# Row-cut transposes in the mixture-of-experts loop: seven of eight transposes of a 64-slot block work on 64 rows

## The reference, cut to what matters

```
for each expert e, over its tokens (rows of h, gathered):
    gu   = xb @ w_e1[e] + b_e1[e]            # 1024 -> 2048
    gate = min(gu[:, :1024], 7);  up = clip(gu[:, 1024:], -7, 7)
    act  = (up + 1) * (gate * sigmoid(1.702 * gate))
    y    = act @ w_e2[e] + b_e2[e]           # 1024 -> 1024
```

## Time and profile before

| | |
|---|---|
| median of 3 runs | 1825.05 us (1824.0 to 1827.08) |
| the profiled execution, its own time | 1826.37 us |
| its span in the trace | 1824.1 us |
| TensorE busy | 1649.4 us (90%), 6773 matmuls and transposes |
| TensorE weight loads busy | 1213.6 us (67%) |
| VectorE / ScalarE busy | 1387.1 us (76%) / 1049.0 us (58%) |
| the chain that ended last | TensorE 62%, VectorE 18%, issue 10%, ScalarE 7% |
| mean granted clock of TensorE | 0.954 |

### The profile page before, as it was taken

How to read it: one execution, slowest core, us unless ns; L and a number is a source line. 1 busy time by engine, 2 the same in 40 slices (tenths; PEclk the granted TensorE clock), 3 DMA queues, 4 the chain that set the end, 5 groups by cost and what they waited for, 6 DMA issues and landing times.

```text
span 1824.1 us, 20657 instructions
## 1 busy us (share of the span) xinstructions
PE 1649.4 (90%) x6773; PEld 1213.6 (67%) x6773; DVE 1387.1 (76%) x1198; ACT 1049.0 (58%) x1038; POOL 313.2 (17%) x301
## 2 busy tenths in 40 slices
PE   2999989988898389999999999999999999999872
PEld 2776667766677367667777776777777766777640
DVE  7878756656547757898889889889889889888626
ACT  2456822556423245677668667767767767766511
POOL 1600000100000102223123132132222312312000
PEclk8999989999998599999999999999999999999985
DMA  8333255312155269999999999999999999999435
GB/s 324 111 139 139 81 179 191 97 47 70 47 215 220 79 245 366 400 408 400 388 402 413 382 391 415 385 384 416 382 373 416 388 375 405 391 378 397 181 146 233
DMA packets 112255, 519.82 MB, mean 285 GB/s; under 512 B 15666, under 2 KB 48978, under 8 KB 57906
## 3 DMA queue, kind: packets, MB, share of 16 engines
q1 hardware_dynamic: 97168, 492.99, 68.8%
q0 software_dynamic: 10208, 17.64, 2.8%
q10 hardware_dynamic: 4834, 8.60, 1.3%
HBM read 514.46 MB, written 19.66 MB: 293 GB/s over the span
## 4 chain that ended last, share of the span: by engine, by line
PE 62%; DVE 18%; issue 10%; ACT 7%; DMA 2%; POOL 2%; ACTq 0%; DVEq 0%; POOLq 0%
PE ps L2125 28%; PE ps L2141 13%; PE ps L1832 9%; DVE lo L1686 7%; PE ps L2042 2%; PE ps L2057 2%; PE ps L2097 2%; ACT hi L1092 2%; POOL gw L622 1%; DVE acc L1235 1%; PE ps L2112 1%; PE ps L1921 1%; ACT hi L860 1%; PE ps L2105 1%; ACT prob L981 1%
## 5 line engine op out<-in xcount | busy, mean ns | idle before, releaser
L1686 DVE TENSOR_TENSOR lo<-raw,hi 128x2048 fp32r<-128x2048 f32 x318 | 716.8, 2285 | 156.5 <-ACT hi L1092 156.5
L1092 ACT ACTIVATE hi<-raw 128x2048 fp32r<-128x2048 f32 x318 | 596.9, 1911 | 231.5 <-PE ps L2125 217.3
L2125 PE MATMUL ps<-hi,x_a 128*128 128x512 f32 x864 | 242.9, 411 | 0.0
L1832 PE MATMUL ps<-hT,hi 128*128 128x512 f32 x704 | 231.4, 404 | 10.4 <-DVE qbd L1445 8.5
L753 POOL TENSOR_TENSOR ticks<-eps 128x1 f32<-128x1 f32 x100 | 75.6, 756 | 738.2 <-ACT ysb L1129 709.2
L2125 PEld LDWEIGHTS ps<-hi,x_a 128*128 128x128 f32 x864 | 162.7, 191 | 42.0 <-issue 9.4
L1832 PEld LDWEIGHTS ps<-hT,hi 128*128 128x128 f32 x704 | 133.5, 190 | 46.5 <-issue 16.2
L2125 PE MATMUL ps<-hi,x_b 128*128 128x512 f32 x480 | 137.1, 407 | 4.0 <-DVE lo L1686 2.8
L1832 PE MATMUL ps<-hT,lo 128*128 128x512 f32 x352 | 138.1, 392 | 0.0
L2141 PE MATMUL ps<-raw,a 128*128 128x512 f32 x288 | 129.4, 592 | 0.0
L2125 PE MATMUL ps<-raw,x 128*128 128x512 f32 x288 | 129.4, 592 | 0.0
(11 more groups left out here) (330 smaller groups left out, 2460.4 us busy)
## 6 DMA issues: line engine op xcount, KB each, us to landing
raw<-w_e_dram SPq DMA_DIRECT2D x396, 1024.0 KB, 8.7
raw<-w_ada_dram SPq DMA_DIRECT2D x24, 1024.0 KB, 6.8
raw<-w_in_dram SPq DMA_DIRECT2D x15, 1024.0 KB, 5.4
raw<-w_merge_gate_dram SPq DMA_DIRECT2D x8, 1024.0 KB, 5.2
yk<-yk_d SPq DMA_DIRECT2D x4, 2048.0 KB, 14.5
raw<-w_branch_rnn_dram SPq DMA_DIRECT2D x8, 640.0 KB, 6.3
raw<-w_branch_attn_dram SPq DMA_DIRECT2D x4, 1024.0 KB, 4.8
raw<-w_out_dram SPq DMA_DIRECT2D x4, 1024.0 KB, 4.8
```

The source lines that it names most:

```text
L1092: s.activation(hi[u.slot(i)][:, :], raw[i][:, :], ACT.Copy).then_inc(hi_done, 1)
L1686: v.tensor_tensor(lo[i][:, :], raw[i][:, :], hi[u.slot(i)][:, :].bitcast(F32), ALU.subtract).then_inc(split_done, 1)
L1832: last = mm(ps[:, bank, :], wk[:, k, c0:c0 + P], acts[xa][:, k0 + k, :], start=start and k == 0 and q == 0, stop=stop and k == kn - 1 and ...
L2125: last = mm(ps[:, q, :], x_, w[:, q * 512:(q + 1) * 512], start=False, stop=i == M1 - 1, skip_group_check=True)
```

## The change

`turn_x` and `turn_a` get the kind of the block as an argument. The first of the eight transposes stays as it was. The other seven take `cap` rows of the data (all 128 columns) as the stationary operand and the upper left `cap` x `cap` corner of the unit matrix as the moving one; `cap` is 128 for an A block, which leaves these as they were, and 64 for a B block. Where kind B stands, the seven write only the 64 columns that are read later.

```
@@ -2090,19 +2090,23 @@
-            def turn_x(n_in):
-
+            def turn_x(n_in, kind):
+
+                cap = CAP_A if kind == "A" else CAP_B
                 pe.wait_ge(xg_in, n_in)
-                for k in range(KT):
-                    last = nc.tensor.transpose(ps[:, 6 + k // 4, k % 4 * P:(k % 4 + 1) * P], xg[:, k * P:(k + 1) * P], ident[:, :])
+                nc.tensor.transpose(ps[:, 6, 0:P], xg[:, 0:P], ident[:, :])
+                for k in range(1, KT):
+                    last = nc.tensor.transpose(ps[:, 6 + k // 4, k % 4 * P:k % 4 * P + cap], xg[0:cap, k * P:(k + 1) * P], ident[0:cap, 0:cap])
                 last.then_inc(xT_ps, 1)
 
-            def turn_a(b):
-
+            def turn_a(b, kind):
+
+                cap = CAP_A if kind == "A" else CAP_B
                 pe.wait_ge(glu_done, b(1, 0))
-                for k in range(KT):
+                nc.tensor.transpose(ps[:, 6, 0:P], act_h[:, 0:2 * P - 1:2], ident[:, :])
+                for k in range(1, KT):
                     c0 = k // 2 * 2 * P + k % 2
-                    last = nc.tensor.transpose(ps[:, 6 + k // 4, k % 4 * P:(k % 4 + 1) * P], act_h[:, c0:c0 + 2 * P - 1:2], ident[:, :])
+                    last = nc.tensor.transpose(ps[:, 6 + k // 4, k % 4 * P:k % 4 * P + cap], act_h[0:cap, c0:c0 + 2 * P - 1:2], ident[0:cap, 0:cap])
                 last.then_inc(aT_ps, 1)
...
@@ -2179,12 +2183,12 @@
                     if i == 1:
-                        turn_a(u.b)
+                        turn_a(u.b, u.down)
...
                         pe.wait_ge(aT_done, u.b(1, 0))
-                        turn_x(u.b(16, 32))
+                        turn_x(u.b(16, 32), next_x)
...
             u = first()
-            turn_up(u)
+            turn_up(u, "B")
...
             with pe.Fori(0, N_PAIRS) as j:
                 u = odd(j)
-                turn_up(u)
+                turn_up(u, "B")
                 turn_down(u)
                 u = even(j)
-                turn_up(u, At(2, j), y=True)
+                turn_up(u, "A", At(2, j), y=True)
                 turn_down(u, At(2, j))
             u = last_turn()
-            turn_up(u, x_late=True)
+            turn_up(u, "A", x_late=True)
```

More of the change, by code:

```diff
@@ L2171, in fold_y, with turn_up @@
                 last.then_inc(ylow_used, 1)
-            def turn_up(u, nb=None, y=False, x_late=False):
+            def turn_up(u, next_x, nb=None, y=False, x_late=False):
                 up_start(u.b)
@@ L2199, in _ @@
             pe.wait_ge(xg_zero, 1)
-            turn_x(16)
+            turn_x(16, "A")
             pe.wait_ge(sel_done, 1)
@@ L2213, in _ @@
                 up_chunk(i, "A", whi)
-            turn_x(32)
+            turn_x(32, "A")
             pe.wait_ge(down_done, 2)
@@ L2217, in _ @@
             u = first()
-            turn_up(u)
+            turn_up(u, "B")
             turn_down(u, first=True)
             u = second()
-            turn_up(u, At(1))
+            turn_up(u, "A", At(1))
             turn_down(u, At(1))
@@ L2241, in _ @@
             b = u.b
-            turn_a(b)
+            turn_a(b, "A")
             turn_down(u)
```

## The result

The changed kernel takes 1830.51 us in the median of 11 runs (1827.3 to 1832.15), the kernel before 1824.91 us in 11 (1822.62 to 1827.08). The ratio is 1.0031, with a 95% interval of 1.0022 to 1.0040: slower by 5.6 us. The profiled execution's span is 1829.9 us, against 1824.1.

A forecast was written before the change was run, and what follows sets the result against it. TensorE was taken to bound the odd turns, where the changed groups lie; 15 x (0.315 for `turn_a` - 0.02 for `turn_x`) = 4.4 us more gave 1829.5 us, about 0.24% slower, range 1820.0 to 1835.0.

The forecast's parts named there:

- The crossings: At each changed group's two borders, between 128-row and 64-row instructions, TensorE drains: 0.20 us each, range 0 to 0.25.
- Inside a group: Six distances between 64-row transposes: `turn_x` saves 0.31 us (0.109 to 0.058 each), `turn_a` 0.02 (0.119 to 0.115).
- the -0.02 of the sum: Net of a changed `turn_x` group: 0.15 going in, 0.31 saved inside, 0.14 coming out, -0.02 us.
- nothing is drained: Rival, at the group borders: crossings cost nothing, so 4.9 us are gained, 1820.1 us; 18%.
- the 64-row loads don't speed up: Rival, inside both groups: distances stay near 0.109 us and crossings cost as forecast, 10 us slower, 1835.1 us; 10%.
- the strided load becomes short with fewer rows: Rival, inside `turn_a`: its load becomes short too, with both crossings; sum -1.6 us, 1823.4 us, no measurable difference; 17%.

The follow-up runs named there:

- alternate_x: Against the kernel before, in `turn_x` of B blocks transposes 1, 3, 5, 7 take 64 rows and the others 128, `turn_a` as before; ratio 1.0090.
- rows66: Against the kernel before, the seven transposes of B blocks take 66 rows and a 66 x 66 unit matrix in both groups; ratio 0.9975.
- deint64: As deint_only, with the seven transposes of B blocks at 64 rows in both groups; ratio to the kernel before 1.0003.
- deint_only: Against the kernel before, VectorE writes even and odd activation columns apart into `sg`, which `turn_a` reads without a stride; all transposes keep 128 rows; ratio 1.0007.

## Why the prediction was right

**Where the bound is.** TensorE is the chain in the odd turn, and what a group costs there arrives in the end: 0.332 us more for a `turn_a` group (1.51 against 1.18) and 0.005 for a `turn_x` group make 0.337, the pair of turns grew by 0.346, and 14 to 15 of them give 5 us of the 5.6 measured. The copy in the first pass is 0.25 us earlier than before, that in the last 4.25 us later, and the span 5.8 us longer: some 1.5 us came behind the loop, of which the `turn_a` group of the last turn explains 0.33. For the rest no cause was looked for; one profiled execution can't tell it from scatter.

**The crossings.** Two per group, 0.20 us from the last full instruction to the first load of the new shape. That was forecast from two places in the attention, seen once each, and stands in the profile after as forecast. alternate_x confirms it with eight crossings in a group (1.035 us against 1.0) and rows66 by taking them away with nothing else changed to speak of. With the rows of the stationary operand the columns of the moving one went from 64 to 66 too; that it is the rows is told by the attention, where a stationary operand of 64 rows shows the pause with 512 moving columns, and one of 128 rows shows none with 64 moving columns (the scores, loads 0.111 us apart). No run tried another number of rows than 64, 66 and 128.

**Inside a group.** `turn_x` was forecast at 0.058 us between loads and came to 0.062; with this the group gives +0.005 us, not the -0.02 of the sum. `turn_a` was forecast at 0.115 and stayed at (0.91 - 0.20) / 6 = 0.118, the pace it had: with the borders +0.332 us instead of +0.315. Both errors made the forecast too low, and they make 15 x 0.042 = 0.6 of the 1.2 us by which the forecast of 4.4 us fell short of the 5.6. The lengths that the prediction gave for whole groups were too long by about 0.1 us: it had 0.95 and 1.3 us for `turn_a` and 0.86 for `turn_x`, up to the next product, where the rows have 0.86 and 1.17, and 0.79 and 0.78. The same 0.1 us stood before and after, so it didn't touch the sum.

**The rivals.** That nothing is drained is refuted by the loads at both borders. That the 64-row loads don't speed up is refuted by the 0.062 us of `turn_x`. That the strided load becomes short with fewer rows is refuted by the 0.118 us of `turn_a`; deint64 shows what would have come of it: the group at 0.79 us to the product, and no difference to before. The rule in the Trainium skill, "TensorE: Matmul & The Clock Gate", section LDWEIGHTS, 107 ns for the load of 128 columns, fits neither group of transposes: 0.062 us between the loads of `turn_x`, 0.118 between those of `turn_a`.

**What the numbers of the prediction rested on.** The rule of "TensorEngine Tiling (Array Packing)", section Tiling Modes, Key Properties, in the Trainium skill, that a change of the tiling mode drains the engine, agrees with this trace where the rows change: the next load starts 0.20 us after the last full transpose began. The narrow transposes of the attention, another shape in columns only, showed no such pause; whether they are a change of mode at all no run here tells.

## What to carry to other kernels

Before cutting a matmul or transpose down to the rows it needs, look at what stands ahead of it and behind: going from 128 rows to 64 and back cost about 0.15 us each way here, by the sum of the prediction that `turn_x` bore out, and that is as much as three short transposes save (0.109 - 0.062 = 0.047 us each). Seven in a row came out even; that 64 rows pay in longer runs of one shape follows from these numbers as an estimate, and no run here has one. Two rows more than the 64 kept the short streaming and showed no pause (0.51 us for the group of `turn_x` in rows66, 0.79 before). And ask first whether load or streaming sets the pace; where a strided stationary operand does, as in `turn_a`, fewer moving columns saved nothing until the stride was gone.

## What was not expected of the hardware

The strided load of `act_h` kept its 0.118 us when the streaming beside it was cut to half, with 64 rows ((0.91 - 0.20) / 6) and no shorter group with 66 (0.87 us to the product against 0.86). I had put it at 0.115 from the shortest loads of the trace, as though the streaming beside it made it longer. Without the stride the same group came to 0.062 us apart, so the stride of two elements about doubled the distance between the loads. And VectorE read its half-size pieces with a stride of two elements (it wrote them without one) at no price that shows: 693 ns each in deint_only, where an instruction of the same kind and size without a stride (L1356) takes 693 in the same kernel. The whole in one instruction took 1221, so what is paid is the second instruction.
